# A two-block transformer on one core: first norm row by a matmul of ones, first weights in four pieces, taps, rotary set-up and x turned at other places

## The reference

```python
def rmsnorm(x, g):
    y = xf * lax.rsqrt(jnp.mean(xf * xf, axis=-1, keepdims=True) + NORM_EPS)
    return y * g
...
hn = rmsnorm(h, norm_g[i])
q, k, v, z = split_proj(hn, w_in)                  # hn @ w_in, 1024 x (2 * 1024 + 2 * kv)
...
h = h + (o * silu(z)) @ w_out[i]
...
ang = positions[..., None] * inv_freq              # second block only: rotary tables
cos, sin = jnp.cos(ang), jnp.sin(ang)
y = conv(u, w) + b                                 # second block only: 4 taps and a bias
```

## Time and profile before

| | |
|---|---|
| runs (us) | 925.25, 920.56, 919.92; median 920.56 |
| profiled execution | 923.07, of which 921.2 is the span from first to last instruction |
| mean granted clock | 0.991 |
| PE busy | 882.9 us (96%) |
| DVE, ACT, POOL busy | 558.5, 518.6, 127.7 us (61, 56, 14%) |
| DMA | 146.88 MB, mean 159 GB/s |
| chain that ended last | PE 70%, issue 21%, DVE 3%, ACT 2%, DMA 2% |

### The profile page before, as it was taken

The page is one execution under the profiler, slowest core; times in us unless marked ns, Lnnn a source line. Parts: engine busy times, 40 slices in busy tenths (PEclk is TensorE's granted clock), DMA queues, the critical chain, the costliest instruction groups (busy, mean ns, idle before and its releaser), DMA issues.

```text
span 921.2 us, 12293 instructions
## 1 busy us (share of the span) xinstructions
PE 882.9 (96%) x4557; PEld 728.8 (79%) x4557; DVE 558.5 (61%) x969; ACT 518.6 (56%) x853; POOL 127.7 (14%) x103
## 2 busy tenths in 40 slices
PE   4899998999999999999999999999999999999995
PEld 3787887878787888788888888887888888888884
DVE  4754578546766567865555544756677755555443
ACT  3567755676487685464444433677874644444331
POOL 0031103421015350000000000042430000000000
PEclk9899999999999999999999999999999999999998
DMA  8641344443544424576565555534423766565521
GB/s 279 218 150 57 129 163 157 140 129 102 177 167 139 137 93 136 164 236 187 188 185 183 183 183 185 193 104 139 137 92 120 246 190 188 186 190 189 196 95 46
DMA packets 94846, 146.88 MB, mean 159 GB/s; under 512 B 6476, under 2 KB 54852, under 8 KB 94788
## 3 DMA queue, kind: packets, MB, share of 16 engines
q1 hardware_dynamic: 91392, 139.14, 46.3%
q0 software_dynamic: 1440, 5.24, 2.0%
q10 hardware_dynamic: 1956, 1.71, 0.5%
HBM read 145.04 MB, written 1.05 MB: 159 GB/s over the span
## 4 chain that ended last, share of the span: by engine, by line
PE 70%; issue 21%; DVE 3%; ACT 2%; DMA 2%; POOL 0%; ACTq 0%; POOLq 0%; DVEq 0%
PE bank L1000 55%; PE bank L975 6%; PE bank L1141 1%; PE bank L1052 1%; PE bank L1055 1%; PE bank L1077 1%; PE bank L1076 1%; DMA taps_stage<-in_conv_b 1%; PE bank L1075 1%; DMA gains<-in_norm_g 1%; ACT junk L1186 1%; DVE lo L901 1%; ACT hi L1161 1%; DVE hyb_MT L1749 1%; PE bank L1120 0%
## 5 line engine op out<-in xcount | busy, mean ns | idle before, releaser
L901 DVE TENSOR_TENSOR lo<-raw,hi 128x1024 fp32r<-128x1024 f32 x246 | 302.4, 1254 | 133.7 <-ACT hi L1161 131.6
L1161 ACT ACTIVATE hi<-raw 128x1024 fp32r<-128x1024 f32 x262 | 268.4, 1056 | 77.0 <-PE bank L1000 69.9
L1000 PE MATMUL bank<-hi,xT_hi 128*128 128x512 f32 (+2 forms) x736 | 294.4, 400 | 8.5 <-DVE lo L901 3.1
L1000 PE MATMUL bank<-hi,xT_lo 128*128 128x512 f32 (+2 forms) x736 | 285.5, 388 | 0.0
L1000 PE MATMUL bank<-lo,xT_hi 128*128 128x512 f32 (+2 forms) x736 | 284.5, 387 | 0.0
L1000 PEld LDWEIGHTS bank<-hi,xT_hi 128*128 128x128 f32 x736 | 140.0, 190 | 41.6 <-issue 13.8
L1000 PEld LDWEIGHTS bank<-hi,xT_lo 128*128 128x128 f32 x736 | 139.6, 190 | 28.9
L1000 PEld LDWEIGHTS bank<-lo,xT_hi 128*128 128x128 f32 x736 | 140.3, 191 | 25.5 <-issue 0.5
L1000 PE MATMUL bank<-hi,hT 128*128 128x512 f32 x352 | 111.2, 395 | 0.0
L1000 PEld LDWEIGHTS bank<-hi,hT 128*128 128x128 f32 x352 | 66.3, 188 | 15.4
L1000 PE MATMUL bank<-lo,hT 128*128 128x512 f32 x176 | 69.4, 395 | 0.0
(11 more groups left out here) (230 smaller groups left out, 983.5 us busy)
## 6 DMA issues: line engine op xcount, KB each, us to landing
raw<-in_w_in SPq DMA_DIRECT2D x26, 1024.0 KB, 5.1
raw<-in_w_gate SPq DMA_DIRECT2D x44, 512.0 KB, 4.0
raw<-in_w_up SPq DMA_DIRECT2D x44, 512.0 KB, 4.9
raw<-in_w_down SPq DMA_DIRECT2D x22, 1024.0 KB, 4.9
raw<-in_w_out SPq DMA_DIRECT2D x20, 1024.0 KB, 5.1
raw<-in_w_in_b SPq DMA_DIRECT2D x10, 1024.0 KB, 5.1
raw<-in_w_in_a SPq DMA_DIRECT2D x8, 1024.0 KB, 7.8
gains<-in_norm_g POOLq DMA_DIRECT2D x2, 512.0 KB, 6.8
```

The lines of the kernel that those rows point to most:

```text
L901: return engine.tensor_tensor(lo[r][:, cols], raw[c.i % RAW][:, cols], hi[r][:, cols].bitcast(F32), ALU.subtract)
L1000: last = nc.tensor.matmul(bank[:, 0:wd], still[a], mv[r][:, off:off + wd], start=c.first and i == 0 and j == 0, stop=c.last and i == len(t ...
L1161: nc.scalar.activation(hi[c.i % SPLIT][:, cols], raw[c.i % RAW][:, cols], ACT.Copy)\
```

## The change

- The first gain row comes as one row of 4 KB into one partition (from ACT's queue, its first instruction). PE spreads it over the partitions by two fp32 matmuls of a row of ones with it (`spread`), into the scratch banks 4 and 5, and `gained` reads it from there. The row of the second norm is loaded by POOL at step rest 4, behind its share of the first norm factor.
- DVE sets `ones`, `warm` and the ones beside v first of all. PE runs 6 + 1 + 4 matmuls of `warm` with itself around the spread and the first turns; their result is never read.
- Chunk 0 is loaded, rounded, subtracted and waited for in four pieces of 512 columns.
- The taps are turned in mixer b (`sc.heads == 32`), behind chunk 16.
- `angles()` is cut into four parts at rest 9, chunk 10, rest 10 and chunk 11; the sine is taken at rest 12; the exp of `small` behind the scores of head 8 in mixer a, where the exp table is loaded; `tables()` at chunk 14.
- Behind mixer b the last quarter of x is turned ahead of the squares and the factor `first`.

The diff, cut to its core:

```diff
-SETUP_AT = 15
+ANGLES_AT = (("rest", 9), ("chunk", 10), ("rest", 10), ("chunk", 11))
+SINE_AT, TABLES_AT, ALOG_AT = 12, 14, 8
+FIRST_ROWS_AT = 4
...
     def second_half():
         turn_x(sc, 1, 0)
         squares(sc, 0)
+
+    def factors():
+        turn_x(sc, 1, 1)
         if mid:
             squares(sc, 1)
             factor(sc, "first")
-
-    def factors():
-        turn_x(sc, 1, 1)
-        if mid:
             normed_residual(sc)
...
-    if sc.heads == 16:
+    if sc.heads == 32:
         bk = sc.bank()
         s = sc.step("taps", bank=bk)
...
+    b0, b1 = sc.bank(), sc.bank()
+    sc.gain_now = {"banks": (b0, b1), "users": [], "made": None, "spread": sc.step("spread", banks=(b0, b1))}
...
-                    for half in range(2):
-                        dst = slot[:, half_of(c, half)].rearrange("p (k n) -> p k n", n=cw)
-                        n = len(ks) // 2
-                        sp.dma_start(dst, wt[:, n * half:n * (half + 1), c0:c0 + cw]).then_inc(raw_in[0] if half else raw_first, 16)
+                    for k in ks:
+                        sp.dma_start(slot[:, k * cw:(k + 1) * cw], wt[:, k, c0:c0 + cw])\
+                          .then_inc(raw_first[k] if k < 3 else raw_in[0], 16)
...
+        pe.wait_ge(warm_up, 1)
+        warmed(6)
         for s in sc.steps:
+            if s.kind == "spread":
+                pe.wait_ge(first_gain_in, 16)
+                for n in range(2):
+                    last = nc.tensor.matmul(freed(pe, s.banks[n])[:, :], ones[0:1, :],
+                                            first_gain[0:1, n * 512:(n + 1) * 512], start=True, stop=True)
+                last.then_inc(sem["spread", "tensor"], 1)
+                pe.wait_ge(const_in, 16)
+                warmed(1)
+            if s.kind == "begin":
+                warmed(4)
...
+        act.dma_start(first_gain[0:1, :], t["norm_g"][0:1, :]).then_inc(first_gain_in, 16)
...
-                if s.kind == "chunk" and s.i == SETUP_AT:
+                if s.kind == "rest" and s.i == SINE_AT:
                     act.wait_ge(setup_dve, 2)
                     nc.scalar.activation(sine[:, :, :, :], angle[:, :, :, :], ACT.Sin).then_inc(setup_act, 1)
-                    nc.scalar.activation(small[:, :, 1, :], small[:, :, 1, :], ACT.Exp).then_inc(setup_act, 1)
...
-        load_gain(sc.gains[0])
...
+            if s.kind == "rest" and s.i == FIRST_ROWS_AT:
+                load_gain(sc.gains[0])
...
-                if s.kind == "chunk" and s.i == SETUP_AT:
-                    angles()
-                if s.kind == "chunk" and s.i == SETUP_AT + 1:
+                if (s.kind, s.i) in ANGLES_AT:
+                    angles(ANGLES_AT.index((s.kind, s.i)))
+                if s.kind == "chunk" and s.i == TABLES_AT:
                     tables()
```

More of the change, by code:

```diff
@@ L676 @@
 PARTS = {
-    "chunk": ("tensor", "scalar", "vector", "gpsimd"), "gained": ("vector",), "turn": ("tensor", "scalar", "vector"),
+    "chunk": ("tensor", "scalar", "vector", "gpsimd"), "spread": ("tensor",), "gained": ("vector",), "turn": ("tensor", "scalar", "vector"),
     "taps": ("tensor", "scalar"), "mid_gain": ("vector",), "square": ("scalar",), "meansq": ("vector", "gpsimd"), "newton": ("vector",), "added": ("vector",),
@@ L724, in build @@
     oT = [keep("oT_hi", [P, 12, S], F32R), keep("oT_lo", [P, 12, S], F32R)]
+    warm, _ = at("warm", [P, 512], BF16, place[0] - 2 * 12 * S * 4)
+    first_gain, _ = at("first_gain", [P, D], F32, place[0] - 2 * 12 * S * 4 + 1024)
     raw = [keep(f"raw{i}", [P, CH]) for i in range(RAW)]
@@ L975, in transpose, with warmed @@
             return nc.tensor.transpose(out, in_, ident)
-        pe.wait_ge(const_in, 16)
-        for s in sc.steps:
+        def warmed(n):
+            for _ in range(n):
+                nc.tensor.matmul(psum[3][:, :], warm[:, 0:P], warm[:, :], start=True, stop=True)
+        pe.wait_ge(warm_up, 1)
+        warmed(6)
+        for s in sc.steps:
+            if s.kind == "spread":
[8 more added lines that the diff above has]
+                warmed(4)
             if s.kind in ("chunk", "rest"):
@@ L982, in _ @@
                     ended(pe, x, "vector")
-                if half == 0:
+                if half == 0 and c.i:
                     split_done(pe, c.i, 0)
@@ L1153, in split @@
             if c.i == 0:
-                act.wait_ge(raw_in[0] if half else raw_first, 16)
-            elif half == 0:
+                cw = c.size // 4
+                for k in (2 * half, 2 * half + 1):
+                    act.wait_ge(raw_first[k] if k < 3 else raw_in[0], 16)
+                    cols = slice(k * cw, (k + 1) * cw)
+                    nc.scalar.activation(hi[0][:, cols], raw[0][:, cols], ACT.Copy)\
+                      .then_inc(sem["chunk", "scalar"] if k % 2 else first_hi, 1)
+                return
+            if half == 0:
                 act.wait_ge(raw_in[c.i % RAW], arrived[c.i])
@@ L1295, in _ @@
                                           bias=shift[:, hd, 1:2]), s)
+                if s.i == ALOG_AT:
+                    act.wait_ge(small_in, 16 * NSMALL)
+                    nc.scalar.activation(small[:, :, 1, :], small[:, :, 1, :], ACT.Exp).then_inc(setup_act, 1)
             elif s.kind == "flip" and s.att["kind"] != "h":
@@ L1463, in split @@
         def split(c, half):
+            if c.i == 0:
+                cw = c.size // 4
+                for k in (2 * half, 2 * half + 1):
+                    dve.wait_ge(*((sem["chunk", "scalar"], half + 1) if k % 2 else (first_hi, half + 1)))
+                    cols = slice(k * cw, (k + 1) * cw)
+                    tt(lo[0][:, cols], raw[0][:, cols], hi[0][:, cols].bitcast(F32), ALU.subtract)\
+                        .then_inc(sem["chunk", "vector"] if k % 2 else first_lo, 1)
+                return
             dve.wait_ge(sem["chunk", "scalar"], 2 * c.i + half + 1)
@@ L1500, in set_up @@
             dve.wait_ge(sinks_in, 16)
-            nc.vector.memset(ones[:, :], 1.0)
             ts(sinks[:, 1, :], sinks[:, 0, :], -1.0, None, ALU.mult)
@@ L1559, in _ @@
                     ended(dve, s.gain["made"], "vector")
+                elif "banks" in s.gain:
+                    ended(dve, s.gain["spread"], "tensor")
                 else:
@@ L1570, in _ @@
                 c = slice(s.n * 512, (s.n + 1) * 512)
-                done(tt(quarter[s.buf][:, :], h[:, s.m, c], gains[:, c], ALU.mult), s)
+                rows = psum[4 + s.gain["banks"][s.n].at][:, :] if "banks" in s.gain else gains[:, c]
+                done(tt(quarter[s.buf][:, :], h[:, s.m, c], rows, ALU.mult), s)
             elif s.kind == "turn":
```

58 lines of the change are left out of this document (36 added, 22 removed).

## The result

| | before | after |
|---|---|---|
| runs of the first comparison (us) | 925.25, 920.56, 919.92, 921.02 | 908.58, 908.09, 911.48, 909.65 |
| median | 920.79 | 909.12 |
| profiled execution, its span | 923.07, 921.2 | 908.58, 906.8 |
| PE busy, DVE, ACT, POOL (us) | 882.9, 558.5, 518.6, 127.7 | 883.6, 556.4, 518.4, 131.3 |

The ratio is 0.9867, with a 95% interval of 0.983 to 0.9905: 1.3% faster. The forecast was 904.8 with a range of 901 to 911. The time is in the range and 4.3 us above the point: of the 15.8 us that were forecast, the medians show 11.7, and some 4 us are to be looked for.

What follows compares the result with a forecast made beforehand. PE's product stream was taken as the bound, busy 96% of the span. The terms -6.0 - 5.6 - 4.5 + 0.5 - 0.2 sum to -15.8 us, giving 904.8 us at the median, range 901 to 911.

Steps and rivals of the forecast that it cites:

- Term 1: The start, up to chunk 1: gain row, warm products and chunk 0 in pieces make it shorter, -6.0 us.
- at 7.0. I take that: At the start: the gain row's spread ends at 7.0 us, by the pace doubling 5.0 us after work begins.
- My bound of -3.3: At the start: the smaller gain if chunk 0's first half runs at half rate, ending at 16.9 instead of 14.1.
- The first rival: At the first chunk: the clock is not up, price 2.7 us, giving 907.5; chance 0.13.
- Term 2: The taps ahead of chunk 3: PE no longer waits for their last transfer or falls to half clock, -5.6 us.
- Some of that slips through: Around chunks 3 to 5: ACT's transfers block it 3.66 us and it is 0.5 less ahead than PE.
- The rival with the blocked queue: Second norm's broadcast among the small transfers blocks ACT's queue; 8 us more makes 914.6. Slower 0.02, milder form 0.07.
- Term 3: The set-up ahead of chunk 17: PE's gap goes and the clock stays up, -4.5 us.
- Term 4: The angles' parts near chunk 11 and POOL's gate delay the chain to the turn at 111.72, +0.5 us.
- Term 5: Behind mixer b: the 1.6 us wait for xT_lo goes, but the queries' rotary work comes next, -0.2 us.
- I take the difference off the median.: Whole kernel: the profiled execution's forecast of 907.3, 2.5 above the median, is carried to the median as 904.8.
- The worst case: Whole kernel: the worst of the terms together, -3.3 - 3.6 - 4.4 + 1.2 + 0 = -10.1, giving 910.5 us.

Runs made afterwards that it cites:

- b_taps: The kernel before with only the taps' turn moved behind the keys' step of mixer b; median 916.04 us, ratio 0.9942.
- a_conv: The changed kernel with the taps' two row transfers issued from ACT's queue four chunks later, with their own semaphore; median 908.13 us.

## Why the prediction was right or wrong

- **The forecast as a whole.** All five places were the right ones, and four of the five terms came out within 0.4 us in the pair of profiles. The time landed in the range, but 4.3 us above the point, and for three reasons: the start, the second term, and the step from one profiled execution to the median.
- **Term 1, -6.0.** The pair of profiles gives -6.3, and this is luck on both sides. The other two profiles with the old start have chunk 1 at 22.97 and 23.04, six with the new one at 19.4 to 20.0: -3.0 to -3.7. The step that failed is "at 7.0. I take that" for the end of the spread. It assumed that the clock rises 5.0 us behind the first work, whatever that work is. In six of seven it had not risen by the end of the spread at 8.05, outside my bound of 7.8, and the first product came at 12.90. (The price of the spread was right: 3.78 for two products at half rate, where 2 x 1.92 was the estimate.) My bound of -3.3 was drawn from chunk 0's first half at half rate, and the term came out at it in size, but by another way: the spread and the turns ran at half rate, and most of chunk 0 at full. The first rival (clock not up, 0.13) is closer to these six than the forecast was.
- **Term 2, -5.6.** Mis-sized: -3.9. Alone, with the old start, it is 5.7, as worked out. "Some of that slips through" was put at 0.1 us; the room of the earlier trace rows was the whole matter. ACT came free 10.3 us behind chunk 1's start instead of 8.5: 1.4 by the longer blocking and 0.4 by its shorter lead, which the forecast had at 0.5. With the 0.4 that DVE's chain costs in any case (b_taps) that is the 2.2 us by which the stretch is longer than in a_conv; PE lost them as 1.4 us in two waits and 0.8 in shorter ones. The rival with the blocked queue named the mechanism (blocking 5.5 instead of 4.1), at a size where it costs no half clock.
- **Term 3, -4.5.** Right for the pair of profiles: mixer b's queries come 4.5 us sooner against the turn ahead of them (-9.45 to -13.96), no gap and no 0.50 between 120 and 160 us. But the half clock in it is not in every execution: the same stall (2.7 to 2.8) brought the clock down in three of four profiles, and in b_taps it did not.
- **Term 4, +0.5.** It was +0.8: the wait ahead of the gate's turn grew from 0.3 to 1.0, where 0.8 stood in the text. The second part did meet POOL's gate (1.32 for two instructions), which was hidden as worked out. For the drain that the Trainium skill counts for a switch of tables (ScalarE: Activation LUTs, "What ACT_TABLE_LOAD costs"), by which 1.0 us more would go, the traces show no sign. Ahead of mixer b's first scores in after, ACT's activation before the load ends at 154.39, the load begins at 154.41 and takes 1.28, and the probabilities' activation begins at 155.70, 0.01 behind it. The third stretch is 0.3 short of the forecast in all, which is about what the gate's wait took beyond it.
- **Term 5, -0.2.** The wait of 1.6 for xT_lo has become one of 0.8 for a lo at the same place; the rotary work of the queries never held PE. From the queries to the hybrid's keys all kernels with the new order take 105.94 to 105.99, those with the old one 106.35 to 106.37: -0.4. The rest of the span takes 654.54 to 654.65 instead of 654.28 to 654.53 (654.74 in the profile of before), so 0.1 to 0.3 is given back there, and about -0.2 is left. What gives it back shows in all nine profiles with the new order, and in none with the old one: a wait of 0.3 for DVE's hyb_acc, at 272.68 in after.
- **"I take the difference off the median."** This step cost most, since it takes for granted that each stall of the profiled execution is in the median one too. The profiled execution of before lay 2.3 above its median. 1.0 of it was in its start (24.05, where two other profiles of that start have 22.97 and 23.04). The other candidate is the half clock behind the set-up's stall, worth 1.5 in the third stretch (109.65 against 108.15 in b_taps): the runs of before with a granted clock like the profile's are 3 us slower than the rest. Which stretch it was in the runs without a profile is not shown. By 23.0 for the old start, 19.6 for the new one and the same stretches otherwise, the sum is -3.4 - 4.1 - 3.8 - 0.2 = -11.5, near the 11.5 to 11.7 of the medians. This is no proof: both the start of 19.6 and the half clock in the -3.8 may be less usual than it takes them to be, and the two would cancel.
- **The bounds.** The worst case adds +1.2 for term 4, whose own bound was +2.2. With that the worst would have been 911.5 and not 910.5. It made no difference here.

## What to carry to other kernels

Start from the room of every engine at the place where a stall is taken away, not from the stall: the engine that issues transfers in its own queue (here ACT, 4 to 6 us) becomes the next wait once PE comes sooner, and the edit that gives the gain is to issue them where they don't block. Follow the chain from that engine to PE: here it ran through 11 us of DVE's work without a gap. Edits interact: in the traces the start alone brought 2.2 us, and 3.4 with the taps out of its way. Before a difference between two profiled executions is believed to 1 us, look at two or three traces of each, and at the granted clock of the runs without a profile: the first clock rise alone moves the time by 1.5, and a half clock that comes in some executions only moves it by as much.

## What the runs showed of the hardware

- Two transfer issues on ACT's queue took 3.3 to 5.8 us right behind six others, between 22 and 32 us, and 0.77 at 50 us. ACT computed nothing meanwhile (6.07 us without work in after).
- An fp32 spread of one row over 2 x 512 columns took 3.8 us in nine of ten profiles and 2.3 in the one where the clock rose in its course.
- The clock: up at 10.9 us with the warm products behind the spread, at 12.3 to 14.4 with six of them ahead of it (once at 5.0, then down over 8.4 to 11.8), at 15.5 with the spread in halves between them, at 17.1 without any. A wait of 1.37 us (616 to 633 us, by kernel) left it at full in 13 profiles and was followed by a half clock in one; a wait of 2.7 to 2.8 us at the set-up was followed by a half clock of 3.4 us in three profiles and not in the fourth.
- DVE's small instructions (128x16) took 0.13 each while POOL was idle, and 0.66 beside POOL's gate.
- ACT's load of an activation table took 1.28 us each time, 0.02 behind the activation ahead of it; where the input was there, the next activation began 0.01 behind the load.
